# First input tiles on ScalarE's DMA queue, norm weight on GpSimd's, and three additions of squares on GpSimd in place of VectorE

## What is computed

```
h = RMSNorm(x) * norm_mix          # x: 320 tokens x 2048
z = h @ w_in                       # one combined projection
# three mixers (sparse attention, block-sparse attention, retention) on z,
# gates, output projection, then a convolutional FFN, final RMSNorm
```

## Time and profile before

| | |
|---|---|
| median of three runs | 2366.3 us (2366.17 to 2366.84) |
| profiled execution | 2366.43 us, of which the span of the core 2364.9 us |
| TensorE busy | 2349.3 us |
| VectorE busy | 1408.7 us |
| ScalarE busy | 921.6 us |
| GpSimd busy | 313.2 us |

### The profile page before, as it was taken

How to read it: one execution, slowest core, us unless ns; L and a number is a source line. 1 busy time by engine, 2 the same in 40 slices (tenths; PEclk the granted TensorE clock), 3 DMA queues, 4 the chain that set the end, 5 groups by cost and what they waited for, 6 DMA issues and landing times.

```text
span 2364.9 us, 44606 instructions
## 1 busy us (share of the span) xinstructions
PE 2349.3 (99%) x17234; PEld 2272.2 (96%) x17242; DVE 1408.7 (60%) x2107; ACT 921.6 (39%) x1283; POOL 313.2 (13%) x629
## 2 busy tenths in 40 slices
PE   9999999999999999999999999999999999999998
PEld 9978999999999999999999999999999999999998
DVE  6535568899987555445456655666654446666443
ACT  5334443433343445434333344333333333333432
POOL 1135110000002232333200011000000000000001
PEclk9999999999999999999999999999999999999999
DMA  8448645556558888999776544444445544444553
GB/s 247 146 131 241 181 146 181 178 169 207 206 173 265 303 296 294 305 341 311 238 267 198 182 152 150 152 152 151 152 148 154 154 151 157 155 147 150 156 154 115
DMA packets 176306, 458.69 MB, mean 194 GB/s; under 512 B 25226, under 2 KB 75002, under 8 KB 175968
## 3 DMA queue, kind: packets, MB, share of 16 engines
q1 hardware_dynamic: 142192, 370.84, 48.3%
q0 software_dynamic: 26128, 75.67, 9.9%
q10 hardware_dynamic: 7776, 9.35, 1.1%
HBM read 425.27 MB, written 27.52 MB: 191 GB/s over the span
## 4 chain that ended last, share of the span: by engine, by line
PE 95%; DVE 1%; ACT 1%; DMA 1%; SPq 1%; issue 1%; DVEq 0%; ACTq 0%
PE ps L801 87%; PE ps L1027 1%; PE ps L1057 1%; PE ps L1090 1%; DMA w_raw<-in_w_in 1%; PE ps L874 0%; ACT w_hi L1146 0%; DMA kix<-in_cache_a_kidx 0%; PE ps L998 0%; SPq L462 0%; PE ps L941 0%; PE ps L990 0%; DVE w_lo L1429 0%; SPq L454 0%; PE ps L977 0%
## 5 line engine op out<-in xcount | busy, mean ns | idle before, releaser
L1429 DVE TENSOR_TENSOR w_lo<-w_raw,w_hi 128x1024 fp32r<-128x1024 f32 (+2 forms) x630 | 750.9, 1194 | 784.2 <-ACT w_hi L1146 781.1
L801 PE MATMUL ps<-h_hi,w_hi 128*128 128x320 f32 x3696 | 1158.6, 313 | 2.3 <-DVE h_lo L1592 1.7
L801 PE MATMUL ps<-h_lo,w_hi 128*128 128x320 f32 x3696 | 1131.5, 306 | 0.0
L801 PE MATMUL ps<-h_hi,w_lo 128*128 128x320 f32 x3696 | 1125.0, 304 | 0.0
L1146 ACT ACTIVATE w_hi<-w_raw 128x1024 fp32r<-128x1024 f32 (+2 forms) x630 | 650.1, 1034 | 801.4 <-PE ps L801 762.8
L801 PEld LDWEIGHTS ps<-h_hi,w_hi 128*128 128x128 f32 x3696 | 694.1, 188 | 29.0 <-issue 23.9
L801 PEld LDWEIGHTS ps<-h_lo,w_hi 128*128 128x128 f32 x3696 | 694.1, 188 | 0.4
L801 PEld LDWEIGHTS ps<-h_hi,w_lo 128*128 128x128 f32 x3696 | 693.7, 188 | 0.0
L801 PE MATMUL ps<-y_hi,w_hi 128*128 128x320 f32 x688 | 213.3, 310 | 0.0
L801 PE MATMUL ps<-y_lo,w_hi 128*128 128x320 f32 x688 | 210.5, 306 | 0.0
L801 PE MATMUL ps<-y_hi,w_lo 128*128 128x320 f32 x688 | 209.2, 304 | 0.0
(11 more groups left out here) (329 smaller groups left out, 2068.7 us busy)
## 6 DMA issues: line engine op xcount, KB each, us to landing
w_raw<-in_w_in SPq DMA_DIRECT2D x250, 512.0 KB, 5.0
w_raw<-in_ffn_up SPq DMA_DIRECT2D x86, 512.0 KB, 4.0
w_raw<-in_ffn_gate SPq DMA_DIRECT2D x86, 512.0 KB, 3.8
w_raw<-in_ffn_down SPq DMA_DIRECT2D x80, 448.0 KB, 3.4
kpg<-in_cache_b_k SPq DMA_DIRECT2D x128, 128.0 KB, 4.4
vpg<-in_cache_b_v POOLq DMA_DIRECT2D x128, 128.0 KB, 4.9
kpg<-in_cache_a_k SPq DMA_DIRECT2D x128, 128.0 KB, 4.3
vpg<-in_cache_a_v POOLq DMA_DIRECT2D x128, 128.0 KB, 4.6
```

The lines of the kernel that those rows point to most:

```text
L801: mm = mmul(bank[q][:, 0:T], wp[:, s, cols], xp[:, x.k0 + k, :], start=(x.first and k == 0 and t == 0), stop=(x.last and k == x.nk - 1 and ...
L1429: tt(w_lo[:, s, 0:n], w_raw[:, s, 0:n], w_hi[:, s, 0:n].bitcast(F32), ALU.subtract).then_inc(w_lo_done, 1)
```

## The change

Three things are done. SP no longer transfers lot 0 of x; ScalarE issues that transfer in the place where it issued the norm weight's. The norm weight's transfer is now the first instruction on GpSimd. And the three additions of squares move from VectorE, where they stood between `low` of units 13 to 15, to GpSimd, behind its constants' transfers; VectorE passes four units in one go and then waits for all three. TensorE's semaphore count goes from 1 to 4, because GpSimd raises the same semaphore three times.

```diff
@@ SP
             transfer(0)
-            features(0)
             features(1)
@@ GpSimd
+            pool.dma_start(gmix[:, :], a["norm_mix"]).then_inc(g_in, 16)
             pool.wait_ge(x_arrived[3], 16)
...
+            for g in range(1, 4):
+                pool.wait_ge(x_sq, g + 1)
+                nc.gpsimd.tensor_tensor(sqx[:, 0:4, :], sqx[:, 0:4, :], sqx[:, 4 * g:4 * g + 4, :], ALU.add).then_inc(x_sqs, 1)
+                pool.wait_ge(x_sqs, g)
             pool.wait_ge(r_made, 1)
@@ TensorE
             dense(17)
-            pe.wait_ge(x_sqs, 1)
+            pe.wait_ge(x_sqs, 4)
@@ ScalarE
-            act.dma_start(gmix[:, :], a["norm_mix"]).then_inc(g_in, 16)
+            act.dma_start(xT[:, X_LOTS[0][0]:X_LOTS[0][1], :], a["x"][:, X_LOTS[0][0]:X_LOTS[0][1], :]).then_inc(x_arrived[0], 16)
@@ VectorE
-            def add_squares(g):
-                dve.wait_ge(x_sq, g + 1)
-                V(tt(sqx[:, 0:4, :], sqx[:, 0:4, :], sqx[:, 4 * g:4 * g + 4, :], ALU.add))
...
             split_features(4)
             dense(2)
-            add_squares(1)
-            dense(1)
-            add_squares(2)
-            dense(1)
-            add_squares(3)
-            dense(2)
+            dense(4)
+            dve.wait_ge(x_sqs, 3)
             V(tt(sqx[:, 0:2, :], sqx[:, 0:2, :], sqx[:, 2:4, :], ALU.add))
             tt(sqx[:, 0, :], sqx[:, 0, :], sqx[:, 1, :], ALU.add).then_inc(x_sqs, 1)
```

## The result

The changed kernel takes 2371.55 us (median of 18 executions, 2370.62 to 2372.67), the kernel before, timed beside it, 2366.59 (18, 2366.10 to 2367.59): 4.96 us more, a ratio of 1.0022 with a 95% interval of 1.0015 to 1.0028. The profiled execution took 2371.43 us, of which the span is 2369.8; 4.9 us over the span before.

A forecast was written before the change was run, and what follows sets the result against it. TensorE, busy 2349.3 of 2364.9 us, was taken to bound the kernel; squares +4.28 and head -0.1 gave +4.2 us, 2370.6 against the profiled execution (2370.5 against the median), range 2365.2 to 2372.6.

The forecast's parts named there:

- One addition between two w_lo: Units 12 to 14: port held, each w_lo waits for one GpSimd addition, 2.84 + 0.61 us a round; chance 0.58.
- The rival in which VectorE runs several w_lo before GpSimd gets its turn: Units 12 to 17: only the first addition delays w_lo, +1.8 us less 0.1, 2368.0 us; chance 0.14.
- the one without holding: Squares' stretch: GpSimd's reads don't stop VectorE, -0.8 us, up to -1.2, 2365.5 us; chance 0.15.
- The absorbed hole: Before unit 15: TensorE's old 0.38 us wait for w_lo disappears, so +4.66 at unit 14 becomes +4.28.
- the 0.38 of unit 15: TensorE's wait before unit 15 at 34.64 in the kernel before, taken off the +4.66 us of unit 14.
- The head: Start up to the first real matmul: earlier x and moved norm weight, -0.1 us, bounds -0.2 and +0.6.
- the sign named for it (behind 7.5): First real matmul behind 7.5 us would show the rival of late loads, +0.6 at most alone; its chance 0.06 ("the rest").
- the two land together: Head: x's 320 KB beside the first weights' 256 KB were taken not to delay the weights.
- it lands at 4.3 to 4.8: Head: the norm weight, issued on GpSimd's queue at about 0.9 us, lands before it is wanted at 5.40; cost nothing.
- the squares' term: Units 12 to 15: three GpSimd additions of 2.84 us holding up VectorE's w_lo, +4.28 us.
- the right rival in the wrong place: From 27 to 38 us TensorE rests and its clock falls, a matmul taking 0.29 us; slower by over 0.2%; chance 0.07.
- Carrying the start to the end at full size: Behind the start TensorE's matmuls pace everything, so a shift of the start reaches the end undiminished.

The follow-up runs named there:

- e1: The changed kernel with its loads put back, so only the additions of squares move to GpSimd; 2371.00 us, ratio 1.0019.
- e2: The kernel before with only the change's three DMA edits, squares staying on VectorE; 2367.16 us, ratio 1.0003.
- e3: The kernel before with x's first lot, then the norm weight, on ScalarE's queue; 2367.23 us, ratio 1.0003.
- e6: The kernel before with only the norm weight's transfer moved to GpSimd's queue; 2367.22 us, ratio 1.0000.
- e7: The kernel before with VectorE's second and third addition of squares one w_lo later; 2366.30 us, ratio 0.9998.
- e9: e1 with each GpSimd addition replaced by two memsets of 128x1280, which only write; 2366.84 us, ratio 1.0001.
- e10: e9 with copies of 128x1280 onto themselves in place of the memsets, reading one operand; 2367.67 us, ratio 1.0004.
- e8: e2 with 15 in place of 10 warm-up matmul calls; 2366.89 us, ratio 1.0000.
- e4: e1 with GpSimd's three additions cut into twelve of 128x320; 2370.69 us, ratio 1.0016.

## Why the prediction was right, and where it was off

**Direction and cause: right.** Forecast +4.2 us, measured +4.96. The step on which it rested, that a VectorE instruction with two inputs in SBUF waits for the whole of a GpSimd addition that began first, is shown by the long w_lo, by their absence with memsets, and by their being cut with the additions. What the earlier trace rows showed in one direction holds in both.

**One addition between two w_lo: right.** The two rounds measured 3.44 and 3.24 us (first matmuls of units 12, 13 and 14 at 30.75, 34.19 and 37.43), forecast 2.84 + 0.61 = 3.45. GpSimd's addition of 128x1280, put at 2.84 from two smaller ones, lasted 2.94 to 2.98 where VectorE wasn't in its way. Unit 14 began at 37.43, forecast 37.2. The rival in which VectorE runs several w_lo before GpSimd gets its turn fell with that, and the one without holding fell with the long w_lo.

**The absorbed hole: right.** Of 4.92 us at unit 14, 4.53 remain at the sum; the 0.38 of unit 15 was taken off.

**The head: wrong.** I took -0.1 and bounded it by -0.2 and +0.6; the first real matmul slipped by 0.97, past the bound, and the sign named for it (behind 7.5) stood in the trace at 7.94. The step that failed is "I take that the two land together": the first weights landed 0.8 us later with x beside them, not at the old time. And "it lands at 4.3 to 4.8" failed twice: GpSimd's queue issued the norm weight at 1.41 and not at 0.9, and it took 5.1 us where I had taken the 3.4 and 3.9 of transfers of a calmer time. Of the 0.97, 0.60 is left at the sum (44.64 against 44.04 in e1). That the forecast survived it is partly luck: the squares' term was 0.35 too large (4.28, in e1 3.93 at the sum, where GpSimd's first addition began at 26.59 and not at 27.05).

**The clock: the right rival in the wrong place.** I feared a fall between 27 and 38 us. There TensorE rested 1.42 and 1.27 us at a time and the clock stayed at 1.00. It fell behind the head, where TensorE had rested from 5.82 to 7.94. The price that I had put on a matmul at the lower level was a little high too: 0.267 us measured, not 0.29.

**The chances: too low on the slower side.** The ratio 1.0022 lies just past the 0.2% that I had named as the bound, with 0.26 given to that side and 0.73 to within. My sum was 0.8 us short. By the column of the sum, 0.7 of it is the head (-0.1, measured +0.60) and 0.4 lies behind the sum, where I had put nothing (4.53 there, 4.96 in the time); the squares' term takes 0.35 off again.

**Carrying the start to the end at full size** is right only to 1 or 1.6 us. Sum and time agree within 0.6 for the change (4.53 and 4.96), e1 (3.93 and 4.49), e2 (0.85 and 0.65), e3 (1.01 and 0.72) and e6 (0.30 and 0.60, though its profiled execution lies 2.2 us above its median); but e7, e9 and e10 were 0.91, 0.97 and 0.40 ahead at the sum and came out at -0.32, +0.34 and +1.17. About 1 us of that goes at the very end. These are the matmuls of `by_token` near the end, as they stand in the chain of waits of before and of e7:

```profile
2354.55 0.95 PE ps L1130 x6
```

```profile
2353.41 1.66 PE ps L1130 x6
```

In e7 they run at the lower clock from the start (its granted clock is 0.68 in the two us from 2352.70, where before has 1.00 in those from 2352.90), and from the first matmul of L1121 to the end of the span it takes 14.1 us in place of 13.1, of which these six matmuls are 0.71. The profiles of e6, e9 and e10 show the same (14.0 to 14.1 us, 1.60 to 1.66 for these six matmuls), all the others 13.0 to 13.2 us. Each is one execution, so whether the earlier start brings this about or chance does, no run says; the rest of the difference lies between the sum and L1121 and stays open.

## What to carry to other kernels

Before work is moved from VectorE to GpSimd, count which VectorE instructions with two SBUF inputs run in the same stretch: each that comes while a GpSimd instruction that reads SBUF runs waits for its end, so the longer GpSimd's instruction is, the longer the wait. Shorter ones hold it up for less at a time, but here they ended so late that nearly as much was lost. An idle engine is no spare capacity if its work shuts out the one that is relieved; here the order of VectorE's own instructions gave at the sum what there was to win, under 1 us, and no gain that the timing could tell. And a transfer that is started beside the first one on the path can delay that one: here x on ScalarE's queue made the first weights 0.8 us later than x behind them on SP's.

## What the runs showed of the hardware that I had not expected

- The first transfer on GpSimd's queue is issued at 1.41 us where SP's and ScalarE's are at 0.88, in all four kernels that have one (the change, e2, e6, e8).
- The norm weight's 8 KB for 128 partitions took 4.0 us on ScalarE's queue (before) and 4.4 on GpSimd's (e6) while x was issued behind the first weights on SP's; with x on ScalarE's queue beside the weights it took 5.1 on GpSimd's (the change, e2, e8) and 5.4 behind x (e3).
- TensorE's rests before the first real matmul and the granted clock behind it: after 0.9 us (e8), 1.2 (e1, e4, e9, e10), 1.45 (e7) and 1.7 us (before) it stayed at 1.00; after 2.1 (e6, the change), 2.5 (e2, e3) and, later, 2.76 (e4) matmuls went for a while from 0.145 to 0.267 us apart. The same ten warm-up calls ahead of the rest took between 3.88 (e6) and 4.64 us (e4, e10), so the rest isn't fixed by the kernel alone.
- On GpSimd an instruction of 128x1280 lasted 1.17 us as a memset, 1.25 as a copy without VectorE in its way, and 2.94 as an addition.
